# Streaming encoder step, float32, one core: summing four of six modulation products on VectorE and GpSimd instead of TensorE

## The reference

```python
def modulation(c, w, b):
    m = jnp.einsum('bd,de->be', jax.nn.silu(c), w) + b
    return jnp.split(m, 3, axis=-1)

def pool_mixer(h, hist, hist_pos, w_in, w_grp, scale, w_out):
    u, gate = jnp.split(h @ w_in, 2, axis=-1)
    pooled, new_hist = multiscale_pool(u, hist, hist_pos)
    z = jnp.einsum('btgc,gcd->btgd', pooled, w_grp).reshape(B, T, POOL_WIDTH) * scale
    y = (z * jax.nn.silu(gate)) @ w_out
    return y, new_hist
```

## Time and profile before

| | |
|---|---|
| time, median of 3 runs | 1630.01 us (1628.29 to 1632.76) |
| the profiled execution, its own time | 1634.17 us |
| its span in the profile | 1632.4 us |
| granted TensorE clock, mean | 0.984 |
| busy: TensorE | 1567.8 us (96%) |
| busy: VectorE | 826.5 us (51%) |
| busy: ScalarE | 729.6 us (45%) |
| busy: GpSimd | 422.4 us (26%) |

### The profile page before, as it was taken

How to read it: one execution, slowest core, us unless ns; L and a number is a source line. 1 busy time by engine, 2 the same in 40 slices (tenths; PEclk the granted TensorE clock), 3 DMA queues, 4 the chain that set the end, 5 groups by cost and what they waited for, 6 DMA issues and landing times.

```text
span 1632.4 us, 26333 instructions
## 1 busy us (share of the span) xinstructions
PE 1567.8 (96%) x9355; PEld 1318.8 (81%) x9355; DVE 826.5 (51%) x2154; ACT 729.6 (45%) x1618; POOL 422.4 (26%) x403
## 2 busy tenths in 40 slices
PE   6899999999999999998989899999999999999997
PEld 3799987788778777888888898888788887888876
DVE  1565434433444344346666634666446664366652
ACT  2444432323332333235555554566435665455643
POOL 0233431112121211112222341333213333123332
PEclk8899999999999999999999999999999999999999
DMA  7787799987998698863222365335463334643323
GB/s 265 273 278 269 245 316 318 346 276 275 316 338 286 248 345 302 301 215 111 98 104 105 117 242 188 129 131 183 151 207 130 129 130 174 210 162 131 131 78 129
DMA packets 174511, 341.97 MB, mean 209 GB/s; under 512 B 22127, under 2 KB 89023, under 8 KB 174126
## 3 DMA queue, kind: packets, MB, share of 16 engines
q1 hardware_dynamic: 174382, 340.29, 60.3%
HBM read 266.13 MB, written 74.31 MB: 209 GB/s over the span
## 4 chain that ended last, share of the span: by engine, by line
PE 81%; DVE 6%; ACT 5%; issue 3%; DMA 3%; POOL 1%; SPq 1%; POOLq 0%; DVEq 0%; ACTq 0%
PE ps_u L950 63%; PE ps_o L1184 4%; PE ps_s L1138 3%; PE ps_t L1157 3%; PE ps_s L950 1%; ACT work L1757 1%; PE ps_s L981 1%; DVE work L1484 1%; ACT ps_u L1656 1%; DVE ps_u L1339 1%; DMA w_raw<-in_pool_w_out_dram 1%; ACT silu_g L1672 1%; PE ps_t L1197 1%; DVE ps_o L1514 1%; DVE silu_g L1368 1%
## 5 line engine op out<-in xcount | busy, mean ns | idle before, releaser
L950 PE MATMUL ps_u<-h_all_hi,w_hi 128*128 128x512 f32 (+2 forms) x1440 | 519.0, 360 | 4.7 <-DVE h_all_lo L1269 4.1
L950 PE MATMUL ps_u<-h_all_lo,w_hi 128*128 128x512 f32 (+2 forms) x1440 | 510.2, 354 | 0.0
L950 PE MATMUL ps_u<-h_all_hi,w_lo 128*128 128x512 f32 (+2 forms) x1440 | 509.9, 354 | 0.0
L950 PEld LDWEIGHTS ps_u<-h_all_hi,w_hi 128*128 128x128 f32 x1440 | 273.7, 190 | 57.7 <-issue 17.4
L950 PEld LDWEIGHTS ps_u<-h_all_hi,w_lo 128*128 128x128 f32 x1440 | 273.7, 190 | 36.3
L950 PEld LDWEIGHTS ps_u<-h_all_lo,w_hi 128*128 128x128 f32 x1440 | 273.7, 190 | 34.4
L1339 DVE TENSOR_TENSOR ps_u<-ps_u,rstd_b 128x512 f32<-128x512 f32 (+1 forms) x180 | 107.2, 596 | 258.6 <-PE ps_u L950 251.2
L1897 POOL TENSOR_TENSOR work<-work,recip 128x512 f32<-128x512 f32 (+2 forms) x136 | 133.0, 998 | 358.8 <-DVE recip L1501 358.8
L950 PE MATMUL ps_u<-y_hi,w_hi 128*128 128x512 f32 (+1 forms) x584 | 211.6, 362 | 5.6 <-POOL y_lo L1876 5.3
L950 PE MATMUL ps_u<-y_hi,w_lo 128*128 128x512 f32 (+1 forms) x584 | 207.0, 354 | 0.0
L950 PE MATMUL ps_u<-y_lo,w_hi 128*128 128x512 f32 (+1 forms) x584 | 206.6, 354 | 0.0
(11 more groups left out here) (218 smaller groups left out, 2263.4 us busy)
## 6 DMA issues: line engine op xcount, KB each, us to landing
w_hi<-w_hi_kept SPq DMA_DIRECT2D x176, 512.0 KB, 4.1
w_lo<-w_lo_kept SPq DMA_DIRECT2D x176, 512.0 KB, 5.3
chunks<-in_ada_w_dram SPq DMA_DIRECT2D x32, 512.0 KB, 6.5
w_hi_kept<-w_hi SPq DMA_DIRECT2D x28, 512.0 KB, 3.4
w_lo_kept<-w_lo SPq DMA_DIRECT2D x28, 512.0 KB, 4.4
w_hi_kept<-fore_hi SPq DMA_DIRECT2D x24, 512.0 KB, 6.7
w_lo_kept<-fore_raw SPq DMA_DIRECT2D x24, 512.0 KB, 7.8
w_raw<-in_pool_w_in_dram SPq DMA_DIRECT2D x16, 512.0 KB, 6.3
```

The lines of the kernel that those rows point to most:

```text
L950: last = nc.tensor.matmul(out, w, x, start=(i == 0), stop=(i == n - 1))
```

## The change

Sixteen chunks (i < `first`) stay on TensorE. For the other 32:
- a chunk is now 128 rows of one `ada_w` part with all 1024 columns, instead of 256 rows with 512 columns (the same 512 KB, from rows of 4 KB each);
- VectorE multiplies the chunk by the prompt condition's value of each partition and adds it to a running sum of 128x1024 (`tensor_scalar` for the first of eight, `scalar_tensor_tensor` for the others);
- GpSimd does so for the sample condition: `tensor_scalar`, and for seven of eight also a `tensor_tensor` that adds;
- the sums lie in the unused one of `x_even` and `x_odd` (`mod_sum`); the first chunk of each eight waits until that buffer's old content has been stored;
- step MT for these four makes 16 matmuls of one column, with the sums as weights and a column of ones, which add up over the partitions; the steps MR of these four are gone;
- SyncE waits for both engines before it loads over a chunk.

```diff
             self.steps.append(("ADA", i))
-            if i % KT == KT - 1:
+            if i % KT == KT - 1 and i < self.first:
                 self.steps.append(("MR", i // KT))
...
-        mod_bank = [ps_u[0][:, :], ps_u[2][:, :]] + [ps_s[:, m % 2, :] for m in range(2, 6)]
+        mod_bank = [ps_u[0][:, :], ps_u[2][:, :]]
         mod_turn = [ps_u[0] if m == 0 else ps_o for m in range(6)]
...
-            eng.wait_ge(ada_done, KT * len(sched.mods))
+            eng.wait_ge(ada_added, KT * len(sched.mods) - first)
+            eng.wait_ge(ada_pooled, KT * len(sched.mods) - first)
...
+        def mod_sum(m, v):
+
+            return x_of(m - 1)[:, 2 * v:2 * v + 2, 0:PART]
...
                 if i >= first + CHUNKS:
-                    sp.wait_ge(ada_done, i - CHUNKS + 1)
+                    sp.wait_ge(ada_added, i - CHUNKS - first + 1)
+                    sp.wait_ge(ada_pooled, i - CHUNKS - first + 1)
+                if i >= first:
+                    k = i % KT
+                    sp.dma_start(landing[slot], I["ada_w"][l, k * P:(k + 1) * P, what * D_MODEL:(what + 1) * D_MODEL]).then_inc(ada_loaded[slot], 16)
+                    return
                 elif LANDING <= i < first:
...
+                        sp.wait_ge(mod_turned, len(sched.mods))
...
-                elif kind == "ADA":
+                elif kind == "ADA" and st[1] < first:
 
                     i = st[1]
                     m, half, pair = i // KT, i % KT // 4, i % 4
-                    if m >= 2 and i % KT == 0:
-                        claim("s", (mod_rows_ready, m + 1))
                     slot, nth = ada_slot(i)
                     pe.wait_ge(ada_loaded[slot], 16 * nth)
...
+                    if m >= 2:
+                        pe.wait_ge(ada_added, KT * (m + 1) - first)
+                        pe.wait_ge(ada_pooled, KT * (m + 1) - first)
+                        for k in range(KT):
+                            for v in range(2):
+                                last = nc.tensor.matmul(mod_turn[m][:, 2 * k + v:2 * k + v + 1],
+                                                        mod_sum(m, v)[:, k // 4, k % 4 * P:(k % 4 + 1) * P], ones[:, 0:1], start=True, stop=True)
+                        last.then_inc(mod_turned, 1)
+                        continue
                     pe.wait_ge(mod_rows_ready, m + 1)
...
+                elif kind == "ADA" and st[1] >= first:
+
+                    i = st[1]
+                    m, k = divmod(i, KT)
+                    p = m - 2
+                    slot, nth = ada_slot(i)
+                    if k == 0 and p == 0:
+                        dve.wait_ge(ada_done, first)
+                        dve.wait_ge(x_squared, TILES + 1)
+                        dve.wait_ge(x_turned, TILES + 1)
+                    elif k == 0:
+                        dve.wait_ge(mid_stored[(p - 1) % 2], 16 * KT * ((p - 1) // 2 + 1))
+                        dve.wait_ge(sq_ready, KT * p)
+                    if k:
+                        dve.wait_ge(ada_added, i - first)
+                    dve.wait_ge(ada_loaded[slot], 16 * nth)
+                    chunk = landing[slot].rearrange("p (a c) -> p a c", a=2)
+                    total = mod_sum(m, 0)
+                    if k == 0:
+                        V.tensor_scalar(total, chunk, c_wide[:, k, 0:1], None, ALU.mult).then_inc(ada_added, 1)
+                    else:
+                        V.scalar_tensor_tensor(out=total, in0=chunk, scalar=c_wide[:, k, 0:1], in1=total, op0=ALU.mult, op1=ALU.add).then_inc(ada_added, 1)
...
+                        if p:
+                            dve.wait_ge(mod_turned, p + 2)
...
+                        if p:
+                            act.wait_ge(mod_turned, p + 2)
...
+                elif kind == "ADA" and st[1] >= first:
+
+                    i = st[1]
+                    m, k = divmod(i, KT)
+                    p = m - 2
+                    slot, nth = ada_slot(i)
+                    if k == 0 and p == 0:
+                        pool.wait_ge(c_ready, 1)
+                        pool.wait_ge(ada_done, first)
+                        pool.wait_ge(x_squared, TILES + 1)
+                        pool.wait_ge(x_turned, TILES + 1)
+                    elif k == 0:
+                        pool.wait_ge(mid_stored[(p - 1) % 2], 16 * KT * ((p - 1) // 2 + 1))
+                        pool.wait_ge(sq_ready, KT * p)
+                    if k:
+                        pool.wait_ge(ada_pooled, i - first)
+                    pool.wait_ge(ada_loaded[slot], 16 * nth)
+                    chunk = landing[slot].rearrange("p (a c) -> p a c", a=2)
+                    total, part = mod_sum(m, 1), mod_sum(m, 2)
+                    if k == 0:
+                        G.tensor_scalar(total, chunk, c_wide[:, k, 1:2], None, ALU.mult).then_inc(ada_pooled, 1)
+                    else:
+                        G.tensor_scalar(part, chunk, c_wide[:, k, 1:2], None, ALU.mult).then_inc(ada_scaled, 1)
+                        pool.wait_ge(ada_scaled, i - first - m + 2)
+                        G.tensor_tensor(total, total, part, ALU.add).then_inc(ada_pooled, 1)
```

More of the change, by code:

```diff
@@ L553, in trunk_kernel @@
         w_hi_ready, w_lo_ready, ada_done = sem("w_hi_ready"), sem("w_lo_ready"), sem("ada_done")
+        ada_added, ada_pooled, ada_scaled = sem("ada_added"), sem("ada_pooled"), sem("ada_scaled")
         prm_turned, prm_ready, c_tanh, c_ready, mod_ready = (
@@ L1111, in _ @@
                     pe.wait_ge(k_prev, n)
-                    first = 0 if p else 1
-                    for b in range(TILES + 1 - first):
-                        last = nc.tensor.transpose(s_flat[:, b * P:(b + 1) * P], kv_t[:, (first + b) * P:(first + b + 1) * P], ident[:, :])
+                    b0 = 0 if p else 1
+                    for b in range(TILES + 1 - b0):
+                        last = nc.tensor.transpose(s_flat[:, b * P:(b + 1) * P], kv_t[:, (b0 + b) * P:(b0 + b + 1) * P], ident[:, :])
                     if p == 0:
```

## The result

The changed kernel takes **1683.29 us** (median of 4 runs, 1681.7 to 1686.99) against 1629.15 us for the kernel before (1627.14 to 1632.76): ratio **1.0322, interval 1.0302 to 1.0341**. Slower, as forecast; 1658 was forecast with 1620 to 1686 as its range, so the time lies near the upper end. The profiled spans are 1680.5 and 1632.4 us, and the difference of 48 is what has to be found.

What follows compares the result with a forecast made beforehand. TensorE, 96% busy, was taken as the bound, with VectorE's queue setting its next unit at group ends. Three quarters from -4 (no blocking) to +39 gave +28: 1662, less 4.2 for the median, 1658; range 1620 to 1686.

Steps and rivals of the forecast that it cites:

- The main term: All four stages: VectorE operations stand still while GpSimd runs a long one; +39 us in all if every meeting is lost.
- (a): Sign in the trace: no line-981 matmuls after 60 us, 128 records of the one-column turn, 3.6 us per turn.
- (b): Sign on VectorE: chunk operation's mean well over 1.22 us, PL's copies and running sums with longest times of 2 us and more.
- (c): Sign on TensorE: new waits for `q_st` at z0, 2 to 5 us in groups 0 and 1; silu waits of 1 us and more.
- (d): Sign in stages 1 to 3: a group longer by 2 to 3 us than before, in place of 2.3 shorter.
- Stages 1 to 3, +21: Every meeting lost: 2.6, 2.6 and 0.1 for three groups plus 1.8 for the turn, 7.1 us a stage.
- three quarters of the way: All stages: the forecast was set at +28 us, this share of the way from -4 (no blocking) to +39 (every meeting lost).
- Stage 0, +18: Stage 0, every meeting lost: +6.1 us per three-chunk group, +4 for group 2, +1.8 for the turn.
- Rival 1: VectorE and GpSimd: no blocking that matters, -4 us, time 1626; chance 0.17.
- rival 2: VectorE takes the chunks without any effect on TensorE: full gain, -17.9 us, time 1612; chance 0.13.
- Rival 3: Every meeting lost, +39 us, and GpSimd late with stage 0's low weight halves, +12: time 1681; chance 0.12.
- the likeliest case: VectorE and GpSimd block each other, half to all of the meetings lost: 1640 to 1672 us; chance 0.58.

Runs made afterwards that it cites:

- The version in two pieces: Changed kernel, but stage 0's chunks on TensorE, the other 24 wholly on VectorE in idler places, each turn split into two eights: 1618.87 us, ratio 0.992.

## Why the prediction was right, and where its sizes were off

- **A chunk on TensorE costs 0.78 us, the turn's balance +1.78.** Right. The version in two pieces gives 4.5 to 4.7 us a stage. What it lacked is the clock: a turn in one piece costs 1.6 us more where nothing waits. In stage 1 of the changed kernel the turn itself is 0.5 longer (4.13 against 3.63), and then 13 matmuls run at half clock (372.4 to 378); in stage 2 the clock doesn't fall.
- **The main term, VectorE and GpSimd blocking each other.** Right in mechanism. Of the signs named, (a) came true, and (b) mostly: the copies reach 2.35, the running sum 3.47, VectorE's chunk has a mean of 1.75 on `x_odd` but stays at 1.28 on `x_even`. Signs (c) and (d) came true for group 1 of each stage, where the wait for `q_st` is 3.5 and the group is longer by 2.6, 2.4 and 2.7 us (2.6 was worked out), and not for group 0: its wait is 0.3, 1.8 and 1.8, and it changed by -0.9, +0.9 and +1.2. Waits for the silu of 1 us and more are there in stage 0 only, 0.7 in the others. The rule of the Trainium skill that the prediction leaned on ("SBUF — State Buffer", section Who interferes with whom) held in this trace also for what it exempts: E1, with one input in PSUM, took its 0.70 at 451.46 under GpSimd's product of 448.07 to 451.95.
- **Where in the group it is lost.** Partly wrong. I put all of it ahead of E1 of g0 (U1 + 10) and none behind; it was U1 + 7.2 there, and from there to the end of PQ(1) 7.4 where 4.95 was taken, since PL(1) was met too. The two errors cancel (U1 + 14.6 and 14.95).
- **Stages 1 to 3, +21 with every meeting lost, -8.4 with none.** Measured 18.6, and by groups it divides so. Groups 0 to 2 of the three stages grew by 8.8 us together, where 15.9 was worked out for every meeting lost and -13.8 for none. So "three quarters of the way" was right for them, though the share was a guess, made with a product for GpSimd that was too short, and a guess that comes true on such a footing is in part luck. Group 3 has no chunk and only the turn's 1.8; it grew by 4.9 and 3.3 in stages 1 and 3, where the clock fell behind the turn, and by 1.6 in stage 2, where it didn't. These 4.5 us more than three turns are a term that the sum did not have.
- **GpSimd's product, 1.1 us.** The mis-sized term: 2.85. It was read from a row of another form of the same instruction. That alone is 1.75 us in each of 32 chunks, 56 us of GpSimd, but taking it away gives back only some 6 us of time. The sum's 2.40 was right.
- **Stage 0, +18.** Measured 31.3, the step that was furthest off. Even with the operations cut to 8 columns it grew by 10.0: the third chunk stands where GpSimd starts a W, and in front of E1 of g1, which makes a bank-freeing step wait 2.4 us that did not wait before. I had reckoned this chunk at 1.2, its length; in the changed kernel it takes 3.40 to 3.45. VectorE's sums bring another 4.1 there and GpSimd's 16.0, the two together 1.2. (The forecast's own terms for a group, 4.4, 2, 1.2 and -0.8, add up to 6.8 and not 6.9.)
- **Rivals.** Rival 1 (-4) and rival 2 (-17.9) are out. Rival 3's 1681 is the time measured, but not its story: in stages 1 to 3 not every meeting was lost, and stage 0 lost by VectorE's queue and the silu; TensorE did not once wait for weights of GpSimd's in the pooling stages, only for the silu and `q_st`. The range reached up to 1686 for this rival's sake, so that 1683 lies inside it is luck: the likeliest case's own range ended at 1672, and stage 0 went past it by another path.
- **SyncE and the DMAs at nothing.** Right, as no wait for a weight or a chunk stands among TensorE's.

The division of the loss of stages 1 to 3 between "blocked" and "VectorE's own length in a full queue" is not clean. Both are there, since cutting either engine's part gives 5 to 8 us a stage, and the version of VectorE alone at the same places is blocked by FW as well. That the turn's own columns, and not the sums' reads or the banks, make the clock fall was not separated; only that two halves with a unit between do not.

## What to carry to other kernels

Price an operation that is added to an engine's queue by who stands behind it and frees something, and by what the neighbouring engine runs at that time, not by its length: 0.2 us of work cost 2.4 us here. Work that leaves TensorE pays in full (0.78 us a chunk) once it stands in stretches where its new engine is idle and no long operation of the neighbouring one meets what stands behind it. The same sums of stages 1 to 3 cost 4.9 to 7.1 us a stage in one arrangement and gave 4.5 to 4.7 in another, by the place, the engine and the turn in two pieces; all 32 chunks as changed cost 3%, and the best kernel, with eight of them left on TensorE, gained 0.8%. Take the duration of an operation from a row with the same form, down to the number of its operations.

## What the runs showed of the hardware that was not expected

- On GpSimd, a float32 multiplication of 128x1024 by a scalar took 2.85 us as one operation (2.77 with a constant) and 1.12 us when an addition of 0.0 was added to the same instruction.
- An operation of VectorE on 8 columns, with its inputs in SBUF, took 2.41 us while GpSimd's subtraction of 2.38, recorded from the same moment (81.33), ran; alone it takes 0.22.
- The granted clock fell from 1.00 to 0.50 for some 3.4 us behind 16 one-column matmuls of 3.5 us in all (498.27), without a wait; in all traces at 36 of 38 such turns, some with a wait close by; at 20 halves of eight, the two of a pair 7 us apart, it stayed at 1.00. After stops of 7 to 10 us the first 13 to 24 matmuls ran at 0.50, too, and soon after one of 1.78 at z0 it fell as well, but not after the one of 3.52 at 489.14.
